# Second token blocks of 32 slots in two guarded parts, and an expert loop from odd to even pair

## The reference

```
hidden = silu(t @ w_gate[e]) * (t @ w_up[e])      # 1024 -> 512
out = out + combine[:, e:e+1] * (hidden @ w_down[e])   # 512 -> 1024
```

## Time and profile before

| | |
|---|---|
| median of three executions | 1487.97 us |
| the profiled execution, its own time | 1482.8 us |
| its span, first to last instruction | 1480.9 us |
| TensorE busy | 1320.8 us, 89% |
| VectorE, ScalarE, GpSimd busy | 581.3, 431.7, 410.2 us |
| loads | 448.04 MB, mean 303 GB/s |
| mean granted TensorE clock | 0.968 |
| instruction queue q8 | 79 packets, 1.29 MB |

### The profile page before, as it was taken

How to read it: one execution, slowest core, us unless ns; L and a number is a source line. 1 busy time by engine, 2 the same in 40 slices (tenths; PEclk the granted TensorE clock), 3 DMA queues, 4 the chain that set the end, 5 groups by cost and what they waited for, 6 DMA issues and landing times.

```text
span 1480.9 us, 20887 instructions
## 1 busy us (share of the span) xinstructions
PE 1320.8 (89%) x7694; PEld 815.7 (55%) x7695; DVE 581.3 (39%) x1234; ACT 431.7 (29%) x693; POOL 410.2 (28%) x190
## 2 busy tenths in 40 slices
PE   7999987889899889998789799789997979889975
PEld 6886775534334389766234334279886853333422
DVE  5598543612112162447214222279007062322224
ACT  4554433211111146443111111145435331111110
POOL 5892643100000067151000000069964710000000
PEclk9999999999999999999899999999999999999998
DMA  7664566999999975518589999976544479999953
GB/s 285 215 201 173 186 228 231 393 402 426 426 428 428 391 283 183 190 58 338 231 344 420 426 422 428 397 269 235 191 150 191 170 321 412 422 416 420 427 221 126
DMA packets 89628, 448.04 MB, mean 303 GB/s; under 512 B 7804, under 2 KB 9768, under 8 KB 70952
## 3 DMA queue, kind: packets, MB, share of 16 engines
q1 hardware_dynamic: 85856, 445.87, 75.4%
q10 hardware_dynamic: 3656, 0.57, 0.3%
HBM read 445.38 MB, written 1.05 MB: 301 GB/s over the span
## 4 chain that ended last, share of the span: by engine, by line
PE 65%; DMA 15%; DVE 9%; issue 4%; POOL 3%; ACT 3%; ACTq 0%; SPq 0%; DVEq 0%; POOLq 0%
PE ps L419 63%; DMA ring_hi<-in_moe_w_up 10%; DMA ring_hi<-in_w_up 3%; POOL WLO L2528 3%; DMA ring_hi<-in_ada_w 1%; ACT WHI L1326 1%; DVE Z L1944 1%; DVE Z L1932 1%; DVE Z L1945 1%; DVE Z L1943 1%; DMA ring_lo<-in_w_ckv 1%; PE ps L884 1%; DMA ring_lo<-in_ret_w_in 1%; DMA ring_lo<-in_w_out 1%; POOL RS L2497 1%
## 5 line engine op out<-in xcount | busy, mean ns | idle before, releaser
L2528 POOL TENSOR_TENSOR WLO<-ring_lo,WHI 128x1024 fp32r<-128x1024 f32 (+1 forms) x154 | 379.3, 2485 | 702.6 <-ACT WHI L1326 700.7
L419 PE MATMUL ps<-ring_hi,Z 128*64 128x512 f32 x1248 | 375.4, 616 | 25.3 <-DMA ring_hi<-in_moe_w_up 14.4
L419 PE MATMUL ps<-ring_lo,Z 128*64 128x512 f32 x1152 | 350.6, 613 | 33.6 <-issue 24.3
L419 PEld LDWEIGHTS ps<-ring_lo,Z 128*64 128x64 f32 x1152 | 111.0, 141 | 248.2 <-issue 234.1
L1326 ACT ACTIVATE WHI<-ring_lo 128x1024 fp32r<-128x1024 f32 (+1 forms) x160 | 165.5, 1048 | 214.1 <-PE ps L419 177.3
L419 PEld LDWEIGHTS ps<-ring_hi,Z 128*64 128x64 f32 x1248 | 119.6, 142 | 153.7 <-issue 147.5
L2195 DVE TENSOR_TENSOR Z<-ps,Z 64x512 f32<-64x512 f32 x48 | 33.1, 689 | 357.4 <-ACT Z L1533 354.2
L1533 ACT ACTIVATE Z<-ps 64x512 f32<-64x512 f32 x48 | 28.4, 591 | 370.4 <-PE ps L419 357.6
L419 PE MATMUL ps<-WHI,HTH 128*128 128x512 f32 x320 | 126.8, 396 | 7.2 <-POOL WLO L2528 3.2
L419 PE MATMUL ps<-WLO,HTH 128*128 128x512 f32 x320 | 125.1, 391 | 0.0
L419 PE MATMUL ps<-WHI,HTL 128*128 128x512 f32 x320 | 125.1, 391 | 0.0
(11 more groups left out here) (299 smaller groups left out, 1719.2 us busy)
## 6 DMA issues: line engine op xcount, KB each, us to landing
ring_lo<-in_ada_w SPq DMA_DIRECT2D x22, 2048.0 KB, 8.1
ring_lo<-in_moe_w_gate SPq DMA_DIRECT2D x16, 2048.0 KB, 12.1
ring_lo<-in_moe_w_up SPq DMA_DIRECT2D x16, 2048.0 KB, 16.5
ring_lo<-in_moe_w_down SPq DMA_DIRECT2D x16, 2048.0 KB, 12.6
ring_hi<-in_moe_w_gate SPq DMA_DIRECT2D x16, 2048.0 KB, 13.6
ring_hi<-in_moe_w_up SPq DMA_DIRECT2D x16, 2048.0 KB, 18.5
ring_hi<-in_moe_w_down SPq DMA_DIRECT2D x16, 2048.0 KB, 16.9
ring_lo<-in_ret_w_in SPq DMA_DIRECT2D x12, 2048.0 KB, 8.1
```

What stands on the lines that cost most here:

```text
L419: return nc.tensor.matmul(o, l, r, start=start, stop=stop, skip_group_check=True)
L2528: nc.gpsimd.tensor_tensor(WLO[:, q, 0:size], slot(r)[:, q * size:(q + 1) * size], WHI[:, q, 0:size].bitcast(F32), ALU.subtract).then_inc(S ...
```

## The change

An expert with 65 to 96 tokens no longer takes a further block of 64 slots, but one of 32 (`STRIP`), in two parts. `early` stands after the gate-ups of the pair: gather with `SELF` (one-hot of the tokens past the 64th), XE, and gate and up in four strips of 32 rows with 256 columns each, silu and H. `late` stands after the down products: turns, down in four strips, weighting and scatter. `more` stays for experts with over 96 tokens and for all of their further tokens. Each part stands under a guard of its own for the pair (table rows 6 and 7), and inside it each expert has its own guard. VectorE's `choose_more` moves into `more`; instead `choose_fits` makes SELF of the next pair at each pair's end. The table has eight rows in place of three. SyncE waits for the new parts too. The loop now runs over q = 0, 1, 2 with pair(q,1) and pair(q+1,0), between pair(0,0) and pair(3,1): four bodies, the two in the loop run three times.

```diff
@@ TensorE @@
+            def early(p, k, a, wg, wu, first):
+
+                e = 2 * p + a
+                fits = pe.value_load(TBL[32 * L:32 * L + 1, 3, bass.ds(e, 1)], min_val=0, max_val=1)
+                c1 = pe.value_load(TBL[32 * L:32 * L + 1, 4, bass.ds(e, 1)], min_val=1, max_val=48)
+                bank = (B_XG, B_TR)[a]
+                with pe.If(fits > 0):
+                    if k == 1:
+                        wait_moe(pe, L, "swt", p + 1)
+                        wait_moe(pe, L, "ws", p + 1)
+                    if first and L:
+                        pe.wait_ge(S("gate_in"), L)
+                    wait_moe(pe, L, "self", e + 1)
+                    for c in range(KC):
+                        for t in range(NT):
+                            for x in (XHR, XLR):
+                                ins = mm(ps[:, bank, STRIP * c:STRIP * c + STRIP], x[t][:, P * c:P * c + P], SELF[:, a, t, 0:STRIP],
+                                         t == 0 and x is XHR, t == NT - 1 and x is XLR)
+                    ins.then_inc(S("f_xg"), 1)
+                    pe.wait_ge(S("f_xe"), c1)
+                    for c in range(KC):
+                        for r, w in enumerate((wg, wg, wu, wu)):
+                            ins = mm(ps[STRIP * r:STRIP * r + STRIP, bank, 0:256], XEF[:, c, :], w[:, c, 256 * (r % 2):256 * (r % 2) + 256], c == 0, c == KC - 1)
+                    ins.then_inc(S("f_gu"), 1)
+                    pe.wait_ge(S("f_h"), c1 + 1)
 ...
+            def late(p, k, a, wd, final):
+
+                e = 2 * p + a
+                fits = pe.value_load(TBL[32 * L:32 * L + 1, 3, bass.ds(e, 1)], min_val=0, max_val=1)
+                c1 = pe.value_load(TBL[32 * L:32 * L + 1, 4, bass.ds(e, 1)], min_val=1, max_val=48)
+                bank = (B_XG, B_TR)[a]
+                with pe.If(fits > 0):
+                    if k == 0:
+                        wait_moe(pe, L, "swt", p + 2)
+                        wait_moe(pe, L, "ws", p + 2)
+                    elif not final:
+                        wait_moe(pe, L, "xe_a", p + 2)
+                        wait_moe(pe, L, "xe_v", p + 2)
+                    for t in range(NT):
+                        mm(ps[:, bank, P + P * t:2 * P + P * t], SELF[:, a, t, :], TURNER[:, t, 0:P], True, True)
+                    by4 = SGF[a].rearrange("p (i c) -> p c i", c=4)
+                    for c in range(4):
+                        for r in range(2):
+                            mm(ps[CAP * r:CAP * r + CAP, bank, STRIP * c:STRIP * c + STRIP], by4[:, c, :],
+                               CST[CAP:P, C_ID + CAP + STRIP * r:C_ID + CAP + STRIP * r + STRIP], True, True)
+                    for t in range(NT):
+                        ins = mm(ps[:, bank, 3 * P:3 * P + 32], SELF[:, a, t, :], TURNER[:, t, P:P + 32], t == 0, t == NT - 1)
+                    ins.then_inc(S("f_tp"), 1)
+                    pe.wait_ge(S("f_ht"), c1)
+                    for c in range(4):
+                        for r in range(4):
+                            ins = mm(ps[STRIP * r:STRIP * r + STRIP, bank, 0:256], HTF[:, c, :], wd[:, c, 256 * r:256 * r + 256], c == 0, c == 3)
+                    ins.then_inc(S("f_y"), 1)
+                    pe.wait_ge(S("f_ye"), c1)
+                    scatter_more()
 
@@ TensorE, pair @@
+                if first:
+                    pe.wait_ge(S("table"), L + 1)
+                with pe.If(pe.value_load(TBL[32 * L:32 * L + 1, 6, bass.ds(p, 1)], min_val=0, max_val=2) > 0):
+                    for a in range(2):
+                        early(p, k, a, wg[a], wu[a], first)
                 if k == 0:
                     if first:
                         pe.wait_ge(S("turner_in"), 2 * L + 2)
@@ -988,14 +1058,17 @@
                     wait_moe(pe, L, "xe_v", 2 * q + 3)
                     gather_quad(1)
                 down_half(banks[0], 1, wd)
-                for a in range(2):
-                    more(p, k, a, wg[a], wu[a], wd[a], final)
+                with pe.If(pe.value_load(TBL[32 * L:32 * L + 1, 7, bass.ds(p, 1)], min_val=0, max_val=6) > 0):
+                    for a in range(2):
+                        late(p, k, a, wd[a], final)
+                    for a in range(2):
+                        more(p, k, a, wg[a], wu[a], wd[a], final)
@@ TensorE, moe @@
-            pe.wait_ge(S("table"), L + 1)
             pair(0, 0, first=True)
-            pair(0, 1)
-            with pe.Fori(1, NE // 4 - 1) as q:
-                pair(q, 0)
+            with pe.Fori(0, NE // 4 - 1) as q:
                 pair(q, 1)
-            pair(NE // 4 - 1, 0)
+                pair(q + 1, 0)
             pair(NE // 4 - 1, 1, final=True)
@@ SyncE @@
             if j == 0:
-                blocks_done[a] = sp.value_load(TBL[0:1, L, 2, bass.ds(e, 1)], min_val=1, max_val=48)
+                blocks_done[a] = sp.value_load(TBL[32 * L:32 * L + 1, 2, bass.ds(e, 1)], min_val=1, max_val=48)
+                fits_done[a] = sp.value_load(TBL[32 * L:32 * L + 1, 5, bass.ds(e, 1)], min_val=1, max_val=48)
             if j < 2:
                 wait_moe(sp, L, "gu", e + 1)
             else:
                 wait_moe(sp, L, "y", e + 2 - a)
             sp.wait_ge(m(L, "x_gu" if j < 2 else "xdone"), blocks_done[a])
+            sp.wait_ge(S("f_gu" if j < 2 else "f_y"), fits_done[a])
@@ VectorE @@
+            def choose_fits(e, a):
+
+                V.tensor_tensor(SELF[:, a].rearrange("p t (k s) -> p t k s", s=STRIP), bc(slots[:, 0:STRIP], [NT, P // STRIP, STRIP], 1, 1),
+                                RANKF[:, :, bass.ds(e, 1)].unsqueeze(3).broadcast_to([P, NT, P // STRIP, STRIP]), ALU.is_equal).then_inc(S("moe_self"), 1)
+            ...
+            def early(e, a):
+
+                fits = dve.value_load(TBL[32 * L:32 * L + 1, 3, bass.ds(e, 1)], min_val=0, max_val=1)
+                c1 = dve.value_load(TBL[32 * L:32 * L + 1, 4, bass.ds(e, 1)], min_val=1, max_val=48)
+                bank = (B_XG, B_TR)[a]
+                with dve.If(fits > 0):
+                    dve.wait_ge(S("f_xg"), c1)
+                    for c in range(KC):
+                        o = ps[:, bank, STRIP * c:STRIP * c + STRIP]
+                        if shift is None:
+                            ins = V.tensor_scalar(XEF[:, c, :], o, gain[:, c:c + 1], None, ALU.mult)
+                        else:
+                            ins = V.tensor_scalar(XEF[:, c, :], o, gain[:, c:c + 1], shift[:, c:c + 1], ALU.mult, ALU.add)
+                    ins.then_inc(S("f_xe"), 1)
+                    dve.wait_ge(S("f_sg"), c1)
+                    V.tensor_tensor(SGF[a], ps[CAP:P, bank, 0:256], SGF[a], ALU.mult).then_inc(S("f_h"), 1)
+
@@ VectorE, pair @@
                 p = 2 * q + k
                 e = 2 * p
-                load = [[dve.value_load(TBL[0:1, L, i, bass.ds(e + a, 1)], min_val=i, max_val=(3, 48)[i]) for i in range(2)] for a in range(2)]
                 hidden(p, k, 0)
                 if first and L:
                     dve.wait_ge(S("gate_in"), L)
                 hidden(p, k, 1)
+                with dve.If(dve.value_load(TBL[32 * L:32 * L + 1, 6, bass.ds(p, 1)], min_val=0, max_val=2) > 0):
+                    for a in range(2):
+                        early(e + a, a)
                 if k == 0:
                     weights_out(p, 0)
                     weights_out(p + 1, 1)
@@ -2227,24 +2393,30 @@
                         choose_next(q)
                 elif not final:
                     quad_out(q + 1, 0, (B_XG, B_TR))
-                for a in range(2):
-                    choose_more(e + a, a, 0, load[0][1] + (e + a))
                 if k == 1 and not final:
                     quad_out(q + 1, 1, (B_XG, B_TR))
                 for h in range(2):
                     y_out(p, k, h)
-                for a in range(2):
-                    more(e + a, a, *load[a])
+                with dve.If(dve.value_load(TBL[32 * L:32 * L + 1, 7, bass.ds(p, 1)], min_val=0, max_val=6) > 0):
+                    for a in range(2):
+                        late(e + a, a)
+                    for a in range(2):
+                        more(e + a, a)
+                if not final:
+                    for a in range(2):
+                        choose_fits(e + 2 + a, a)
 
@@ VectorE, table @@
                 ada_add(n)
 
-            for b in range(1, 4):
-                ins = V.tensor_scalar(TBF[0:1, b, :], TBF[0:1, 0, :], b * CAP + 0.5, None, ALU.is_gt)
+            for a in range(2):
+                choose_fits(a, a)
+            V.tensor_reduce(HALF, ident.rearrange("p (h r i) -> p r h i", h=2, r=2), mybir.AxisListType.XY, ALU.add)
+            if L == 0:
+                for i, name in enumerate(("f_gu", "f_y", "f_h")):
+                    V.memset(TBF[0:1, 14, i:i + 1], 0.0).then_inc(S(name), 1)
+            for b, over in enumerate((CAP, CAP + STRIP, 2 * CAP, 3 * CAP)):
 ...
```

(15 more changed lines are left out.)

161 lines of the change are left out of this document (122 added, 39 removed).

## The result

The changed kernel takes **1601.22 us** (median of four runs, 1596.39 to 1608.39) against 1486.95 before: a ratio of 1.078, 95% interval 1.0751 to 1.0808. The prediction was 1643, with a range from 1480 to 1690, and A, code reloaded in each pass, was its forecast.

A forecast was written before the change was run, and what follows sets the result against it. Two clocks bound each pair, loads at about 29.5 us and TensorE at 25.8, with TensorE's program late at five borders. Terms +201 + 21 - 30 - 25 - 14 + 7 = +160 on 1482.8 gave 1643 us, range 1480 to 1690.

The forecast's parts named there:

- A: The forecast case: TensorE's loop code is fetched again in each pass, 1643 us, q8 over 140 packets; chance 0.58.
- jumps over `early`: After each pair's gate-ups, TensorE skips two bodies, 1.6 packets; late where entering new packets, 5.9 us each, 71 in all.
- jumps over `late` and `more`, away from back edges: After the down products, TensorE skips 2.4 packets and always enters two new ones; 16 at 5.9 us, 94 in all.
- six back edges with the jump ahead of each: TensorE's loop end, two a layer, landing on code long gone: +21 us, plus 5.9 for each jump ahead; 56.
- old late borders go: The kernel before's five late pair borders, where TensorE's own program was late, disappear: -30 us.
- waits for loads: TensorE's waits for loads inside pairs go, -18 us, and the slow gate-up behind four of them, -7: -25.
- two blocks: Expert 1 of layer 1 and expert 13 of layer 2 take the new path: 19 us each for 26.4, -14.
- The 35 us of the own range: Allowance subtracted from 1643, with 15 for small errors, to give the own range's lower end, 1593.
- ScalarE's and VectorE's code at nothing: Their jumps fall within their waits of several us and cost nothing; without that cover, some 3 us a pair more.
- B: Rival: code is kept over all passes, only first passes are late; 1530 us (1500 to 1550), chance 0.20.
- C: Rival: long jumps cost no more than cheap borders, up to 1 us; 1459 us (1445 to 1470), chance 0.14.
- D: Rival: effects all but cancel, B's events with early ones hidden or half-price jumps; 1468 to 1498 us, chance 0.08.

The follow-up runs named there:

- a_odd: Changed kernel, TensorE alone without `more` and without `early` and `late` of even experts; 1506.0 us, 1.0151 of the kernel before.
- b_dead: Kernel before plus never-run code on TensorE, 400 instructions after the gate-ups and 280 at the pair's end, under guards; 1679.4 us, 1.1309.
- m_forward: Separate TensorE-only kernel: 33 never-true guards over bodies of 64 to 1024 instructions in straight code; 18 branches took 0.24 to 0.41 us, 15 took 3.30 to 3.87.
- m_loops: Separate TensorE-only kernel: three-pass loops with straight bodies of 512 to 2560 instructions, and bodies with jumps; a pass took 163.8 us for 1536, 273.1 for 2560.
- a_others: Changed kernel with TensorE's whole code, ScalarE and VectorE without `more` and without `early` and `late` of even experts; 1594.1 us, 1.0723 of the kernel before.
- a_lean: Changed kernel, TensorE, ScalarE and VectorE all without `more` and without `early` and `late` of even experts; 1468.6 us, 0.9873 of the kernel before.
- b_onehop: b_dead with the 280 never-run instructions and both `more` bodies under one guard, one jump replacing three; 1613.9 us, 1.0862 of the kernel before.

## Why the prediction was right, step by step

The mechanism was right: TensorE's loop body no longer fits what it keeps, and its jumps meet code that is not there. a_odd shows it in one edit (95 us back), b_dead from the other side. The size was 160 predicted against 116.9 measured (1482.8 to 1599.67, the profiled execution of after; 114.3 by medians). Sizes, in us:

| step | predicted | measured in the trace after |
|---|---|---|
| jumps over `early` | 12 x 5.9 = 71 | 12 gaps, 31.6 in all |
| jumps over `late` and `more`, away from back edges | 16 x 5.9 = 94 | 15 gaps of 37.2, one second gap of 3.7, slow gate-ups 17.1 |
| six back edges with the jump ahead of each | 6 x 5.9 + 21 = 56 | gaps 63.1, slow gate-ups 14.1 |
| old late borders go | -30 | -30, all five gone |
| waits for loads | -25 | -25; one of 4.0 in layer 1 stays, as taken |
| two blocks | -14 | +1 |
| VectorE's table | +7 | at most 1.3, all that changed outside the stretches |
| sum | +160 | +114, and 3 in none of these rows |

- **The price of a jump** was the term that was off. I took the 5.9 of five borders of before for all. Behind `early` the gap is 2.6 on average, and there is no gate-up behind it to slow down. At odd pairs' ends in layers 0 and 1 it is 1.06 to 1.56, since the branch takes only 3.4 to 3.9 and the sequencer is ahead by most of it. In layer 2 the same jump costs 3.69 to 4.13 and a slow gate-up. Over the 27 gaps the mean is 2.55 us, where five borders of before had 4.05.
- **The count** of late `early` jumps came out as 12, but as 8, 4 and 0 by layer, where I had 5, 3 and 4, so that the sum is right by luck. Three of layer 0's eight are landings just ahead of a border: the branch row at 331.1 is 0.45 long, and the gap before 337.64 comes a few instructions behind it, as in m_forward, and ends 2.4 after the q8 packet of 335.21. Two smaller gaps of this kind stand in layer 2, outside the 12: 0.81 at 1309.97 and 1.77 at 1370.27, each ending 2.4 us after a q8 packet began. They are about the size of the 3 us that the table lacks. The 15 of my 16 late jumps at pairs' ends are luck too. Behind the three at a layer's end no gap marked "issue" is over 0.3 us, and two that I had not counted stand in for them, behind the blocks (first and third row; the second is the gap of 1.77):

```profile
810.02 8.97 PE L429 MATMUL ps<-ring_lo,Z 128*64 128x512 f32 x32 [4.65 <-issue]
...
1370.27 0.59 PE L429 MATMUL ps<-YHS,SELTS 128*128 128x512 f32 x1 [1.77 <-issue]
...
1553.31 9.38 PE L429 MATMUL ps<-ring_lo,Z 128*64 128x512 f32 x32 [2.02 <-issue]
```

  By my count the numbering of the packets drifts by about a third of a packet from layer 0 to layer 2; no row shows that. A forecast of single landings from it is not to be trusted, and how many there are came out here by errors that cancelled.
- **Back edges** I put at 4.05 more than a jump. They cost more: a late jump and a late back edge follow each other at once, 12.9 us for both with the slow gate-up, where two terms gave 9.4.
- **The 35 us of the own range**, for late jumps that packets kept in the middle of the body would save, is shown by no run. In m_loops the bodies from 1792 instructions on fetched every packet again in each pass, and in the changed kernel the branch over `late` and `more` at the loop's odd pair lasts 3.4 to 6.4 us in all three passes of each layer.
- **The block** gained nothing. The rows of its products in layer 1, and the windows view of the gate and up there:

```profile
773.82 6.55 PE L429 MATMUL ps<-ring_hi,Z 128*32 128x256 f32 x64 [1.94 <-DVE Z L2272]
...
796.62 3.54 PE L429 MATMUL ps<-ring_hi,Z 128*32 128x256 f32 x32 [2.76 <-ACT Z L1674]
...
803.43 0.66 PE L429 MATMUL ps<-YHS,SELTS 64*128 64x512 f32 x2 [3.27 <-DVE YLS L2303]
```

```profile
773.80:780.40 6.60, 6.55 (x64) 2.90 (x64) 0.00 (x0) 0.00 (x0) 0.00 (x0) 0.55 0.00 0
```

  Four strips do run side by side (6.55 us at 0.55 of the full clock would be 3.6 at the full one, an estimate from this row, and I had put 8.4 if they did not), but the granted clock was 0.55 there and 0.53 in the down products of `late` (796.6 to 800.2): 6.55 and 3.54 where I took 3.5 and 1.7. Early took 14.6 (767.05 to 781.67), late 13.3 (792.03 to 805.37), 27.9 against 26.4; the block of layer 2 is 26.6 against 27.0. I had taken full clock for products that stand between waits. The old gate-up of the block, at 8.44 and not 7.09, should have warned me.
- **ScalarE's and VectorE's code at nothing** was right here (7 us, a_others), but for a reason I did not give: it hides behind TensorE's own wait. Take that cover away and it is 37.
- **Signs.** q8 over 140: 161. Gaps at the same places in all passes: yes. Loads under 380 GB/s: 349, 343, 313. Expert stretches of 280 to 330: 272, 294, 291, one short of it. Gaps marked "issue" of 3 us and more: 13, not about 40; there are 33 of them from 1 us on, a third of them behind gate-ups. A gap behind late jumps of under 2 us was to prove me wrong: at odd pairs' ends in layers 0 and 1 it is (six gaps of 1.06 to 1.56), behind `early` and in layer 2 it is not, and the mean is 2.55. What was wrong at these six was the price, not the cause.
- **Rivals.** B (kept code, late only in first passes) is out, since the gaps and back edges are the same in all passes. C (cheap long jumps, 1445 to 1470) is out for this kernel, and so is D (1468 to 1498). As C has it, the packet begins soon after the branch in m_forward (0.9 to 1.6 us), but the engine goes on only 2.3 to 2.7 later, and the gaps here are 2.55 on average. a_lean's 1468.6 lies in C's range, in part by chance: C counted on 14 us from the blocks, and they gave 4. What holds is that a time below the kernel before was there once the code fits.

What TensorE keeps is told by m_loops: 1536 instructions (6 packets, 7 with the borders, and one ahead) are kept, 1792 are lost whole, with 9 packets of q8 in each pass.

## What to carry to other kernels

Code that hardly ever runs costs by standing in the loop. Count a loop body in packets, rare bodies included, before making the rare case faster. In m_loops a packet held about 256 instructions (in the body of 2560 one came every 27.3 us by the median, at 0.107 us an instruction), and up to 1536 on TensorE nothing was fetched again, from 1792 on everything was in each pass. What costs then are the jumps of more than a packet (all twelve over 512 and more in m_forward waited 3.3 to 3.9), and most of all a back edge right behind one (both together 12.9 us with the slow gate-up); a straight body of 2560 lost nothing in m_loops. One guard over all rare bodies is better than several hops in a row (65 us between b_dead and b_onehop). Look at the compare-and-branch rows first when a gap is marked "issue".

## What the runs showed of the hardware

- A branch to code that is there takes 0.07 to 0.5 us, one to code that is not 3.3 to 3.9 in a quiet kernel (in m_forward q8 starts 0.9 to 1.6 after the branch, and 2.3 to 2.7 later the engine goes on). In the transformer the second part is 2.3 to 2.8 at L1029 and L1061 of the changed kernel, 2.4 in most of them, but the first is mostly either 0.9 to 2.2 or 3.4 to 4.4. In the longer case the packet often starts within 0.3 us of the end of the last product (302.08 and 302.05). What decides between the two is open, and no run was made for it.
- A late back edge right behind a late landing takes 5.05 and 5.09 in m_loops, 7.1 to 8.2 in the transformer.
- VectorE keeps a loop of 195 instructions (the sequencer goes on 0.25 to 0.28 us after the three back edges of before) and loses one of 333 (6.1 to 6.7 us at six of them in a_odd), by my count of its program.
- TensorE's clock fell in a gather of 32-column products. Windows view of a_lean's block, two pieces of the gather and the start of its gate and up:

```profile
714.90:718.00 3.10, 3.10 (x27) 3.06 (x25) 0.69 (x1) 0.59 (x1) 0.00 (x0) 0.89 1.00 428
718.00:720.00 2.00, 1.79 (x9) 1.68 (x8) 0.17 (x1) 0.00 (x0) 0.00 (x0) 0.50 0.37 156
...
721.70:725.00 3.30, 3.28 (x32) 1.59 (x36) 0.00 (x0) 0.00 (x0) 0.00 (x0) 0.50 0.02 5
```

  TensorE was busy throughout the first two pieces, 3.10 of 3.10 and 1.79 of 2.00 us, with short products, and its granted clock went from 0.89 to 0.50 within the gather. It had worked without a break since 706.2.
